# The layer norm and the norm after the second feed-forward take their root and reciprocal over all token columns

## What is computed

```
h += 0.5 * rmsnorm(swiglu(rmsnorm(h)))            first feed-forward (norms pre0/pre4 and post1)
m  = three gated branches of rmsnorm(h)           mixer (norm pre1); branch C has a layer norm ("ln"):
     yc = silu(layernorm(conv31(glu) + b) * g + b)
h += rmsnorm(m @ w_o)                             (post2)
h += 0.5 * rmsnorm(swiglu(rmsnorm(h)))            second feed-forward (pre2 and post3)
h += rmsnorm((p @ w_ple_proj) * sigmoid(rmsnorm(h) @ w_ple_gate))    (pre3 and post4)
```

## Time and profile before

| | |
|---|---|
| median of 3 runs | 1560.54 us (1560.27 to 1561.61) |
| the profiled execution | 1561.8 us, of which its span is 1560.0 us |
| TensorE busy (matmul) | 1544.0 us, 99% of the span |
| VectorE busy | 1044.0 us, 67% |
| ScalarE busy | 697.3 us, 45% |
| GpSimd busy | 613.3 us, 39% |
| mean granted TensorE clock | 0.996 of full speed |

### The profile page before, as it was taken

How to read it: one execution, slowest core, us unless ns; L and a number is a source line. 1 busy time by engine, 2 the same in 40 slices (tenths; PEclk the granted TensorE clock), 3 DMA queues, 4 the chain that set the end, 5 groups by cost and what they waited for, 6 DMA issues and landing times.

```text
span 1560.0 us, 28032 instructions
## 1 busy us (share of the span) xinstructions
PE 1544.0 (99%) x10462; PEld 1532.0 (98%) x10462; DVE 1044.0 (67%) x1619; ACT 697.3 (45%) x1019; POOL 613.3 (39%) x646
## 2 busy tenths in 40 slices
PE   9999999999999999999999999999999999999997
PEld 8999999999999999999999999999999999999997
DVE  6655437999876755534885553399997776555366
ACT  6333434445456433434553333354555554334344
POOL 2855201499330655500046550026963308554000
PEclk9999999999999999999999999999999999999999
DMA  6444432444433544542334454334344435445320
GB/s 217 164 159 175 175 128 83 162 158 143 158 136 109 194 151 148 216 148 81 124 135 161 141 205 149 118 110 162 137 162 144 139 117 189 149 173 185 138 81 35
DMA packets 52344, 228.51 MB, mean 146 GB/s; under 512 B 3760, under 2 KB 3888, under 8 KB 47920
## 3 DMA queue, kind: packets, MB, share of 16 engines
q1 hardware_dynamic: 51696, 225.16, 40.8%
q10 hardware_dynamic: 576, 2.39, 0.5%
HBM read 224.49 MB, written 3.04 MB: 146 GB/s over the span
## 4 chain that ended last, share of the span: by engine, by line
PE 93%; DVE 3%; issue 2%; ACT 0%; POOL 0%; DVEq 0%; POOLq 0%
PE ps L394 29%; PE ps L396 29%; PE ps L395 29%; PE ps L432 1%; PE ps L436 1%; PE ps L433 1%; DVE h L1041 1%; PE ps L493 1%; DVE x_lo L1050 1%; PE ps L565 1%; DVE ssq L1010 0%; PE ps L470 0%; DVE ga L1036 0%; PE ps L462 0%; DVE w_lo_sb L996 0%
## 5 line engine op out<-in xcount | busy, mean ns | idle before, releaser
L996 DVE TENSOR_TENSOR w_lo_sb<-raw,w_hi_sb 128x1024 fp32r<-128x1024 f32 (+1 forms) x390 | 554.1, 1422 | 229.7 <-ACT w_hi_sb L700 228.6
L394 PE MATMUL ps<-x_hi,w_hi_sb 128*128 128x320 f32 x2232 | 693.3, 311 | 0.5 <-DVE w_lo_sb L996 0.5
L395 PE MATMUL ps<-x_lo,w_hi_sb 128*128 128x320 f32 x2232 | 689.6, 309 | 0.0
L396 PE MATMUL ps<-x_hi,w_lo_sb 128*128 128x320 f32 x2232 | 689.6, 309 | 0.0
L700 ACT ACTIVATE w_hi_sb<-raw 128x1024 fp32r<-128x1024 f32 (+1 forms) x388 | 428.7, 1111 | 560.4 <-PE ps L396 468.4
L394 PEld LDWEIGHTS ps<-x_hi,w_hi_sb 128*128 128x128 f32 x2232 | 419.0, 188 | 2.9 <-issue 1.0
L395 PEld LDWEIGHTS ps<-x_lo,w_hi_sb 128*128 128x128 f32 x2232 | 419.1, 188 | 0.6
L396 PEld LDWEIGHTS ps<-x_hi,w_lo_sb 128*128 128x128 f32 x2232 | 419.0, 188 | 0.0
L1421 POOL TENSOR_TENSOR gb<-ga,gb 128x320 f32<-128x320 f32 x88 | 79.8, 906 | 416.2 <-DVE gb L1107 416.0
L395 PE MATMUL ps<-mid_lo,w_hi_sb 128*128 128x320 f32 x704 | 217.4, 309 | 0.0
L394 PE MATMUL ps<-mid_hi,w_hi_sb 128*128 128x320 f32 x704 | 217.4, 309 | 0.0
(11 more groups left out here) (180 smaller groups left out, 1593.4 us busy)
## 6 DMA issues: line engine op xcount, KB each, us to landing
raw<-in_w_f_up SPq DMA_DIRECT2D x86, 1024.0 KB, 5.2
raw<-in_w_f_dn SPq DMA_DIRECT2D x32, 1408.0 KB, 6.1
raw<-in_w_gate SPq DMA_DIRECT2D x24, 1024.0 KB, 5.2
raw<-in_w_out SPq DMA_DIRECT2D x12, 1024.0 KB, 5.2
raw<-in_w_glu SPq DMA_DIRECT2D x8, 1024.0 KB, 5.1
raw<-in_w_short SPq DMA_DIRECT2D x8, 1024.0 KB, 5.2
raw<-in_w_wo SPq DMA_DIRECT2D x8, 1024.0 KB, 5.2
raw<-in_w_pg SPq DMA_DIRECT2D x8, 1024.0 KB, 5.2
```

Source lines behind the costliest of these rows:

```text
L394: pe.matmul(out, whi, rhs_hi, start=start, stop=False, skip_group_check=True)
L395: pe.matmul(out, whi, rhs_lo, start=False, stop=False, skip_group_check=True)
L396: return pe.matmul(out, wlo, rhs_hi, start=False, stop=stop, skip_group_check=True)
L996: dve.tensor_tensor(w_lo_sb[:, j, 0:n], raw[:, j, 0:n], w_hi_sb[:, j, 0:n].bitcast(F32), ALU.subtract).then_inc(w_lo, 1)
```

## The change

Both norms go from the narrow to the wide form. For "ln": TensorE makes `wide_sums` behind j = 2 and nothing behind j = 3; ScalarE takes the root of 128 x 320 into `pmf`, which the mean no longer needs; VectorE takes the reciprocal of `pmf` in place, at the spot where it took the small one; L1333 reads `pmf` in SBUF and not `bc` in PSUM. For "post3": `wide_sums` in place of `sums`, no `spread` behind project 2; root and reciprocal in `rb`, and the steps of the boundary (L1036) read `rb`. `invert_all` moves ahead of `boundary` in the text.

```diff
-        SPREAD = ("post1", "ln", "post2", "post3", "pre3", "post4")
-        WIDE = (None, "pre1", "pre2")
+        SPREAD = ("post1", "post2", "pre3", "post4")
+        WIDE = (None, "pre1", "ln", "pre2", "post3")
...
             def wide_sums(L, name):
-                pe.wait_ge(summed, v_sq(L, name, DT - 1))
+                pe.wait_ge(summed, v_sq(L, name, (WT if name == "ln" else DT) - 1))
                 pe.matmul(bc, ones[:, :], ssq[:, 0:T], start=True, stop=True).then_inc(stat_full, 1)
...
-                pair_of_x(L, "gate2", 0, v_moved(L, "gate2", 0), {2: sums, 3: spread}, "ln")
+                pair_of_x(L, "gate2", 0, v_moved(L, "gate2", 0), {2: wide_sums}, "ln")
...
-                sums(L, "post3")
+                wide_sums(L, "post3")
                 project(2)
-                spread(L, "post3")
...
             def wide_root(L, name):
                 act.wait_ge(stat_full, v_stat(L, name))
-                act.activation(rb[:, :], bc, ACT.Sqrt, bias=eps[:, 0:1], scale=1.0 / D).then_inc(root_ready, 1)
+                e, scale = (eps[:, 1:2], 4.0 / D) if name == "post3" else (eps[:, 0:1], 1.0 / (W if name == "ln" else D))
+                act.activation((pmf if name == "ln" else rb)[:, :], bc, ACT.Sqrt, bias=e, scale=scale).then_inc(root_ready, 1)
...
-                finish_root(L, name)
+                (wide_root if name in WIDE else finish_root)(L, name)
                 split(*nxt, 3)
...
                         act.preload_act_table(ACT.Sqrt)
-                        finish_root(L, "ln")
+                        wide_root(L, "ln")
                         act.preload_act_table(ACT.Sigmoid)
...
+            def invert_all(L, name):
+                dve.wait_ge(root_ready, v_stat(L, name))
+                row = (pmf if name == "ln" else rb)[:, :]
+                dve.reciprocal(row, row).then_inc(rinv_ready, 1)
...
-                    dve.tensor_tensor(STEP[i % len(STEP)], (f if n < 3 else gate)[:, i, :], bc, ALU.mult).then_inc(step_t, 1)
+                    dve.tensor_tensor(STEP[i % len(STEP)], (f if n < 3 else gate)[:, i, :], rb[:, :] if post in WIDE else bc, ALU.mult).then_inc(step_t, 1)
...
-                invert(L, post)
+                (invert_all if post in WIDE else invert)(L, post)
                 if n == 2:
                     keep_product(L, 2)
...
-                dve.wait_ge(bc_full, v_bc(L, post))
+                if post in WIDE:
+                    dve.wait_ge(rinv_ready, v_stat(L, post))
+                else:
+                    dve.wait_ge(bc_full, v_bc(L, post))
...
                     if j == 3:
-                        invert(L, "ln")
+                        invert_all(L, "ln")
...
-                dve.wait_ge(bc_full, v_bc(L, "ln"))
+                dve.wait_ge(rinv_ready, v_stat(L, "ln"))
                 for t in range(WT):
-                    dve.tensor_tensor(cc[:, t, :], cc[:, t, :], bc, ALU.mult).then_inc(ln_step, 1)
+                    dve.tensor_tensor(cc[:, t, :], cc[:, t, :], pmf[:, :], ALU.mult).then_inc(ln_step, 1)
```

More of the change, by code:

```diff
@@ L1087, in boundary @@
                     split(L, "pg", 1, 0)
-            def invert_all(L, name):
-                dve.wait_ge(root_ready, v_stat(L, name))
-                dve.reciprocal(rb[:, :], rb[:, :]).then_inc(rinv_ready, 1)
             def keep_norm(L, n, pre, ph):
```

## The result

The changed kernel takes 1565.02 us (median of 9 runs, 1563.18 to 1566.44), the kernel before 1560.53 (9 runs, 1560.04 to 1561.61). The ratio is 1.0027, 95% interval 1.0018 to 1.0035: slower by 4.2 us (2.8 to 5.5; the medians lie 4.5 apart). The likeliest case had +1.3 us. Laid on the forecast's starting point of 1560.54, the ratio gives 1564.8, which is the upper end of the range; the median itself is 0.2 above that end. It is where rival 1 had put the time. The profiled execution took 1565.53 us with a span of 1563.7, 3.7 more than before.

A forecast was written before the change was run, and what follows sets the result against it. TensorE was taken to bound the kernel at "ln", VectorE at post3. Two layers of 1.55 us lost less 0.90 gained made +1.3 us on the median 1560.54: 1561.8 us, range 1559.2 to 1564.8.

The forecast's parts named there:

- likeliest case: Both norms, two layers: 2 x (1.55 - 0.90) = +1.3 us, median 1561.8 us; chance 54 in 100.
- the range: Whole kernel: 1559.2 to 1564.8 us, taking in a single clock fall and most of the other alternatives.
- rival 1: New TensorE wait at post3: the clock falls, 1562.8 to 1568.4 us; chance 22 in 100 for at least one fall.
- The frame: An edit's value depends on the stretch: TensorE alone without a gap ("ln"), or VectorE feeding it (post3).
- "ln", TensorE: Layer norm: 1.44 us of sums and spread removed, one wide matmul of 0.54 added; gain 0.90 us per layer.
- "ln", the rest: Layer norm, other engines: all that follows the multiplication 0.45 us later, hidden with about 0.3 us left, costed at nothing.
- Rival 2: At "ln", out2 waits for GpSimd's low part and the gain is lost: +1.3 to +3.1 us; chance 10 in 100.
- Post3, VectorE's lateness: Post3: VectorE's first step 1.45 us late, eight steps 0.12 dearer; +1.55 us per layer at the sums of pre3.
- my bounds of 1.3 and 1.75: Post3 loss per layer: 1.3 with the copy hidden and steps no dearer, 1.75 with copy 0.49, steps 0.03 each.
- The port rule: Both norms: VectorE's two-SBUF-input instructions exclude GpSimd, 4 us a layer if it worked beside them; chance 2 in 100.
- The sum without the clock: Both norms, two layers, clock fall costed at nothing: 2 x (1.55 - 0.90) = +1.3 us.
- Rival 3: Post3's delay absorbed by the eight steps or the later stretch to post4: -1.8 us, 1558.7; chance 12 in 100.

The follow-up runs named there:

- the single kernels: Two kernels, each with only one of the two norms changed to wide: the layer norm 1559.90 us, post3 1566.91 us.
- the timed kernel with the filled wait: The changed kernel plus 13 matmuls of no use in TensorE's wait before the sums of pre3: 1562.04 us, ratio 1.0009 to the kernel before.
- post3 alone: The changed kernel with the layer norm put back to the narrow form, only post3 wide: 1566.91 us, ratio 1.0040 to the kernel before.
- the late kernel: The kernel before, norms unchanged, plus two reciprocals of no use on VectorE behind that of post3: 1566.17 us, ratio 1.0037 to the kernel before.

## Why the prediction was right or wrong, point by point

**The frame held.** Two kinds of stretch, TensorE's own at "ln" and VectorE's at post3, and the two norms with opposite signs: the single kernels gave -1.1 and +6.0 us.

**"ln", TensorE: gain 0.90, measured 0.79 and 0.82.** The removed pieces were right, with 0.05 more on the matmul behind the spread. The wide matmul adds 0.70 us here, with nothing on the matmul behind it (0.15), and not 0.54. Its weight load waits 0.2 us for VectorE's last sum of squares, as that of the narrow sums did, and these too were dearer here than at post3 (0.72 against 0.56); that the wait is the cause is read from these rows and was not tried. I took its price from a place without a wait and that of the sums from one with it.

**"ln", the rest: hidden, as said.** GpSimd's last low part ends at 445.57 + 1.77 = 447.34, the first product of out2 starts at 447.91:

```profile
445.57 1.77 POOL L1575 TENSOR_TENSOR y_lo<-cc,y_hi 128x320 fp32r<-128x320 f32 x2 [4.03 <-ACT y_hi L936]
```

```profile
447.91 0.31 PE L394 MATMUL ps<-y_hi,w_hi_sb 128*128 128x320 f32 x1
```

That leaves 0.57 us of slack where I had 0.3. Rival 2 falls. VectorE's chain came 0.3 late and not 0.45: in the timeline the root starts at 432.61, 0.57 ahead of before, which is the shift at the start, and the multiplication at 436.71, only 0.28 ahead.

**Post3, VectorE's lateness: +1.55 in the sum, measured 1.36.** The root and the reciprocal came as priced:

```profile
731.97 2.15 DVE L1019 RECIPROCAL rb<-rb 128x320 f32<-128x320 f32 x1 [0.61 <-ACT rb L718]
734.38 0.47 DVE L1041 TENSOR_TENSOR ga<-f,rb 128x320 f32<-128x320 f32 x1
```

The first step starts 734.38 - 730.67 = 3.71 us behind the start of the wide matmul, where it was 2.36 behind the sums: 1.35 later, for 1.45. The copy of product 2 was dearer in my sum than it is (0.22 on the path), and the eight steps with an operand in SBUF were no dearer: 0.47 to 0.49 us, as before, so my 0.12 is nothing. In sum 1.36 at the sums of pre3 for 1.55, inside my bounds of 1.3 and 1.75.

**The port rule.** GpSimd has no instruction between 700 and 760 us in the changed kernel either, and the multiplications at "ln" end before its next one. The steps at 0.48 us agree with what the prediction took from the Trainium skill, "SBUF — State Buffer", on the shared port pair, as far as GpSimd at rest goes; no run here puts the two engines side by side at these places.

**The sum without the clock: +1.3, measured +1.1** in the profiles (2 x 1.36 less 0.79 and 0.82) and in the timed kernel with the filled wait.

**Rival 1 is what happened, and its chance was the step that failed.** The sum put the clock in the new wait at nothing; it measured +3.1 us. That the range all but holds the time is luck: it was drawn for no more than a single fall, there were two in the profile, and each cost little enough for both to fit. The sign that the prediction gave for this, a granted clock below 1 between 753 and 760 us, is there, and the loss of 4.2 us is beyond the 3.1 that it took as the sign of a missed mechanism. The mechanism, the place and the wait's length were named, as a rival: 2.4 us were expected, 1.9 to 2.2 found. I gave 22 in 100 for at least one fall, with the argument that 246 to 249 us had been as thin and kept its clock. The row on the other side, 769 to 772, carried more, as it turned out: there, as here, the rest stands next to sums of one column, which 246 to 249 us doesn't have. Whether these sums matter was not tried. The prediction also counted only one fall in the kernel before; its clock is at 0.79 and 0.87 in the stretches 5 to 10 and 10 to 15 us as well, at the start of the program. In the changed kernel's profile the clock fell in both layers, in that of post3 alone in one, in that of the late kernel in both: 5 times of 6. The price per fall, 1.54 and 1.57 us, lies inside my 1.0 to 3.3. It can be worked out from rows: 3.4 us at half clock, with matmuls 0.27 us apart in the chain and not 0.15, lose 3.4 x (1 - 0.15 / 0.27) = 1.5. The Trainium skill, "TensorE: Matmul & The Clock Gate", in the part on oscillation, describes a kernel in which a wait behind every burst of matmuls takes the clock down every time. The trace agrees that a wait can do it, with five waits of six; it has one such wait per layer and not a row of them, and one of the six did nothing.

The falls do not come in every execution that was profiled: the one at post4 is in five of the nine profiles of the study. That is likely a part of the spread of every kernel's runs. The changed kernel's runs lie 3.3 us apart, but the kernel before has as much in its longer series (3.8 us in 21 runs, 3.6 in 27), so the spread is no sign of the new wait.

**Rival 3 falls**: nothing took the 1.36 us back.

## What to carry to other kernels

Moving a small statistic to the wide form trades TensorE's instructions for one long reciprocal on VectorE; here it paid where TensorE runs without a gap and VectorE has slack (0.8 us a layer in the chain, though the timed gain of 1.1 us just touches no change), and cost where VectorE's next step opens a stage. When an edit makes TensorE wait, count the wait twice: once as lateness, and once as a possible fall of the clock in the dense work behind it, which here was the larger part (some 2.8 of 4.2 us). If the wait can't be removed, fill it with matmuls that nobody reads, a little shorter than the wait; here that gave back 3.0 us.

## What the runs showed that I had not expected

A single wait of 1.7 to 1.9 us, followed by 0.8 us of matmuls with one output column, was enough to halve the clock for 3.4 us, in five of six cases, with dense work on both sides. Behind the two shorter waits at post4 (0.5 and 0.4 us in the kernel before, between groups of small matmuls) it fell in five of nine profiles. VectorE's reciprocal takes 0.18 us for 3 columns, 0.50 for 64, 0.92 for 128 and 2.15 for 320, about 6.2 ns a column. And the copy of 0.43 to 0.49 us, taken off VectorE's path, gave back only 0.22, as it had overlapped both of its neighbours.
